# A two-layer encoder trunk on one Trainium2 core: FFN stages in pairs of units with half-contraction weight pieces, and mixer projections with 512 moving columns

## The chip, the cores and the metric

The kernel runs on one core of one Trainium2 chip. The metric is the device time of one execution in microseconds (us). Data starts and ends in HBM. The core's engines work side by side and meet at semaphores: TensorE (PE in the profile, its weight loads PEld), VectorE (DVE), ScalarE (ACT), GpSimd (POOL), SyncE (SP). DMAs are issued here by SyncE (weights) and GpSimd (the conditioning matrices).

## What is computed

One sequence of 256 tokens of 1024 features goes through two layers. Each layer is FFN, mixer, FFN; each of the six sub-layers is

```python
cond = silu(c)
mod = (cond @ ada_w[layer] + ada_b[layer]).reshape(B_, 9, D)   # shift, scale, gate of three sub-layers
h = modulate(rmsnorm(x, norm_g), shift, scale)
x = x + gate * sublayer(h)                                     # 0.5 * gate for an FFN
# swiglu(h): a, b = split(h @ w13); (silu(a) * b) @ w2         w13: 1024 x 5632, w2: 2816 x 1024
```

The mixer of layer 0 projects `h` to six segments of 512 columns (`h @ w_in`), runs differential attention (4 heads) and neighbourhood attention (8 heads) and projects back (`@ w_out`, 1024 x 1024). The mixer of layer 1 takes window means over the tokens and multiplies four groups with 256 x 256 matrices. Everything is float32.

## The kernel before

Weights stream once from HBM; activations stay on the chip. A float32 product is made of three matmuls with rounded operands: an operand v is split into `hi` (a rounded copy, by ScalarE) and `lo` (v - hi, by VectorE), and TensorE adds hi*hi, hi*lo and lo*hi (`three`). All weights and activations of FFNs and projections go through this split: `split_hi`/`split_lo` for w13, w_in, w_out and pool_w, `w2_high`/`w2_low` for w2, `u_high`/`u_low` for the product of the FFN's gate.

An **FFN** works in 22 units of 128 hidden columns. `w13` of a unit: for both halves a and b of w13 and the 8 slices k of the contraction, the 128 x 128 weight block is stationary and the transposed activations `hT` move, 256 tokens: 48 matmuls with 256 columns. a goes to columns 0 to 255 and b to 256 to 511 of PSUM bank 4 + Q % 2. Then ScalarE makes silu(a) (`silu`), VectorE multiplies by b (`u_mul`), both split the product (`u_high`, `u_low`), and `w2` of the unit adds into banks 0 to 3: 12 matmuls with 512 columns. TensorE's order is w13 of unit Q, then w2 of unit Q - 1.

Weights arrive by pairs of units. `raw13` has two slots of 2 MB; a pair's two DMAs (1 MB each, both units, all 8 slices) are issued by SyncE once both units of the pair before the last are split (`lo13_done`). `raw2` has two slots of 0.5 MB; SyncE issues w2 of a unit once the slot's last content is split (`lo2_done`). SyncE's queue is in order: pair, w2, w2, pair, w2, w2. `hi13`/`lo13` and `hi2`/`lo2` have two buffers each. The 22 units are one unit, a turn of four written out, four more turns of an engine loop (`Fori`), and the last unit. Each engine's order within a unit is fixed: ScalarE does `silu`, `w2_high`, `u_high`, `split_hi`; VectorE does `u_mul`, a tile, `u_low`, a tile, `w2_low`, `split_lo`.

The **conditioning vectors** (18, `mod`) are matrix-vector products made by VectorE: eight tiles per vector of 128 x 1024 floats (`ada_tile`, 0.5 MB of DMA each, issued by GpSimd into a ring of four), summed over the partitions by eight transposes on TensorE (`mod_sum`) and a reduction (`mod_out`). Two vectors stand ahead of FFN 0, five are made in each of FFN 0, 1 and 2, one in the mixer, none in FFN 3. The gate is turned into a row over all partitions by a diagonal (`diag`, VectorE), a matmul with ones (`gate_row`) and a copy (`gate_copy`); in the FFNs this stands at the end. The last two w2 tiles and the residual of each FFN are interleaved.

**Norms**: ScalarE squares, GpSimd's power, VectorE's scaling, transposes on TensorE, shift and scale on ScalarE into `h32`, split by VectorE (`norm_split`) slice by slice, `hlo_done` counting slices.

**Mixer of layer 0**: twelve units of 256 columns of w_in (`proj`, 48 matmuls with 256 columns: here a token block of `hT` is stationary and the weights move), both token tiles in one bank, banks 4 and 5 in turn, read out by ScalarE (`win_evac`). Squares, sums, norms, tables and rotations of q and k are woven between the units, and heads 0 to 2 of attention A between the last three. w_out is four such units; the first is cut into four parts around the last heads.

The lines that set the order of one turn before:

```python
# SyncE (turn)                       # TensorE (body)
wait lo13_done; 2 x 1 MB of w13      w13(s, Q, n0 + 1 + d, i4)
wait lo2_done; w2                    if with_mod and d == 3: mod_sum(m0, i)
wait lo2_done; w2                    w2(Q - 1, i4, ...)
```

## Time and profile before

| | us |
|---|---|
| three runs: median (lowest to highest) | 1084.23 (1082.85 to 1085.43) |
| profiled execution: first to last instruction | 1077.9 |
| TensorE busy (modelled ends) | 979.4 |
| VectorE busy | 733.9 |
| ScalarE busy | 441.3 |
| GpSimd busy | 123.6 |

The profiled execution's own time is its span of 1077.9 us; what lies around it in a timed run, starting and ending the program, is the difference of 6.3 us to the median. Rows name engine, source line, operation and the tiles written and read; `x48` is a count. Idle time in brackets names the instruction that ended it. Matmuls overlap, so the distance between two starts, not the duration, is what a matmul takes from TensorE. In the chain of waits each step is followed back to what released it. `raw<-in_ff_w` stands for transfers of w13 and of w2 alike.

### The profile page before, as it was taken

Reading aid. Unit: us, or ns where it says so; the run is one execution under the profiler, and the core shown is the slowest. Engines: PE = TensorE matmul, PEld = TensorE weight load, DVE = VectorE, ACT = ScalarE, POOL = GpSimd, SP = SyncE. Lnnn points to the kernel's source line nnn. Section 1 sums busy time; section 2 is a strip of 40 time slices with the busy share of each in tenths; the row PEclk is TensorE's granted clock in tenths of the full one; section 3 lists DMA queues with packets and bytes.
Section 4 is the critical chain, followed back from the end, with each engine's and each line's share of the span. In section 5 each row is a group of like instructions: output and inputs, shape, how many; then the busy total and the mean of one; then the engine's idle time right before and its main releaser. Section 6 shows DMA issues by size and latency. Waiting matters only on the chain.

```text
span 1077.9 us, 17128 instructions
## 1 busy us (share of the span) xinstructions
PE 979.4 (91%) x6656; PEld 893.6 (83%) x6656; DVE 733.9 (68%) x843; ACT 441.3 (41%) x578; POOL 123.6 (11%) x182
## 2 busy tenths in 40 slices
PE   1598999998979898999999989989999879999998
PEld 1487899997969458998998969879989769999997
DVE  4966778678887544875867867668677675555544
ACT  1424343335536343543444444234333544443432
POOL 1110111102541101110101011101110010000000
PEclk9999999998989699899999989999999989999999
DMA  9986888886734022787887747868787416456441
GB/s 339 343 309 229 277 297 297 290 217 223 242 104 131 1 98 98 269 287 284 282 302 262 270 158 257 308 232 307 277 291 275 149 42 235 164 188 202 148 156 39
DMA packets 155690, 239.19 MB, mean 222 GB/s; under 512 B 14464, under 2 KB 124928, under 8 KB 155520
## 3 DMA queue, kind: packets, MB, share of 16 engines
q1 hardware_dynamic: 135056, 166.81, 46.0%
q0 software_dynamic: 19440, 71.31, 18.2%
q8 instruction: 29, 0.48, 0.2%
q10 hardware_dynamic: 1152, 0.49, 0.2%
q14 instruction: 13, 0.11, 0.0%
HBM read 237.54 MB, written 1.05 MB: 221 GB/s over the span
## 4 chain that ended last, share of the span: by engine, by line
PE 42%; DMA 25%; DVE 18%; issue 6%; ACT 5%; SPq 3%; POOL 1%; ACTq 0%; DVEq 0%; POOLq 0%
PE ps L1106 25%; DMA raw<-in_ff_w 24%; DVE lo L703 6%; DVE acc L744 4%; PE ps L1148 3%; PE ps L1147 3%; PE ps L1151 3%; SPq L296 2%; PE ps L1258 2%; DVE lo L709 1%; DVE x L793 1%; ACT arena L487 1%; PE ps L1261 1%; DVE xn L789 1%; ACT hi L455 1%
## 5 line engine op out<-in xcount | busy, mean ns | idle before, releaser
L1106 PE MATMUL ps<-hT_hi,hi 128*128 128x256 f32 x1408 | 402.0, 286 | 11.1 <-DVE lo L703 6.6
L1106 PE MATMUL ps<-hT_lo,hi 128*128 128x256 f32 x1408 | 400.5, 284 | 0.0
L1106 PE MATMUL ps<-hT_hi,lo 128*128 128x256 f32 x1408 | 400.3, 284 | 0.0
L1106 PEld LDWEIGHTS ps<-hT_hi,hi 128*128 128x128 f32 x1408 | 272.2, 193 | 19.4 <-DVE lo L703 10.5
L1106 PEld LDWEIGHTS ps<-hT_lo,hi 128*128 128x128 f32 x1408 | 272.4, 193 | 2.7
L1106 PEld LDWEIGHTS ps<-hT_hi,lo 128*128 128x128 f32 x1408 | 272.2, 193 | 0.0
L703 DVE TENSOR_TENSOR lo<-raw,hi 128x2048 fp32r<-128x2048 f32 (+1 forms) x110 | 243.8, 2216 | 16.2 <-ACT hi L455 15.5
L455 ACT ACTIVATE hi<-raw 128x2048 fp32r<-128x2048 f32 (+1 forms) x106 | 200.2, 1889 | 31.2 <-DMA raw<-in_ff_w 17.5
L511 ACT ACTIVATE hi<-raw 128x1024 fp32r<-128x1024 f32 x88 | 93.4, 1061 | 276.6 <-DMA raw<-in_ff_w 142.7
L720 DVE TENSOR_TENSOR u_lo<-u_buf,u_hi 128x256 fp32r<-128x256 f32 x88 | 37.3, 424 | 212.6 <-ACT u_hi L504 212.5
L744 DVE SCALAR_TENSOR_TENSOR acc<-ada,cond,acc 128x1024 f32<-128x1024 f32 x115 | 147.0, 1279 | 0.7
L1147 PE MATMUL ps<-hi,u_hi 128*128 128x512 f32 x344 | 138.5, 402 | 1.6 <-DVE u_lo L720 1.6
L1148 PE MATMUL ps<-lo,u_hi 128*128 128x512 f32 x344 | 135.5, 394 | 0.0
L387 POOL DMA_DIRECT2D ada<-in_ada_w x112 | 59.4, 530 | 461.6 <-DVE acc L744 345.0
L709 DVE TENSOR_TENSOR lo<-raw,hi 128x1024 fp32r<-128x1024 f32 x88 | 107.2, 1218 | 0.0
L1151 PE MATMUL ps<-hi,u_lo 128*128 128x512 f32 x344 | 106.7, 391 | 0.0
L499 ACT ACTIVATE s_buf<-ps 128x256 f32<-128x256 f32 x88 | 33.6, 381 | 171.9 <-PE ps L1106 171.7
L1106 PE MATMUL ps<-hi,hT_hi 128*128 128x256 f32 x272 | 80.2, 295 | 5.3 <-DVE lo L703 4.3
L1106 PE MATMUL ps<-lo,hT_hi 128*128 128x256 f32 x272 | 78.0, 287 | 0.0
L1106 PE MATMUL ps<-hi,hT_lo 128*128 128x256 f32 x272 | 77.8, 286 | 0.0
L1151 PEld LDWEIGHTS ps<-hi,u_lo 128*128 128x128 f32 x344 | 64.9, 189 | 14.4
L1147 PEld LDWEIGHTS ps<-hi,u_hi 128*128 128x128 f32 x344 | 65.4, 190 | 13.7 <-DVE u_lo L720 2.0
(126 smaller groups left out, 891.2 us busy)
## 6 DMA issues: line engine op xcount, KB each, us to landing
raw<-in_ff_w SPq DMA_DIRECT2D x86, 1024.0 KB, 7.6
ada<-in_ada_w POOLq DMA_DIRECT2D x132, 512.0 KB, 6.7
raw<-in_ff_w SPq DMA_DIRECT2D x92, 512.0 KB, 8.5
raw<-in_w_in SPq DMA_DIRECT2D x12, 1024.0 KB, 8.0
arena<-in_ada_w SPq DMA_DIRECT2D x4, 1024.0 KB, 18.8
raw<-in_w_out SPq DMA_DIRECT2D x4, 1024.0 KB, 6.3
raw<-in_ada_w SPq DMA_DIRECT2D x2, 1024.0 KB, 15.0
arena<-in_b_rpb SPq DMA_DIRECT2D x16, 128.0 KB, 4.2
```

The lines of the kernel that those rows point to most:

```text
L387: pool.dma_start(ada[:, j % ADA_RING, :], ada_v[layer][:, j, bass.ds(i * D + m0 * D, D)]).then_inc(ada_in[j % ADA_RING], 16)
L455: nc.scalar.activation(hi, src, ACT.Copy).then_inc(hi13_done, 1)
L499: nc.scalar.activation(s_buf[:, Q % 2, :], ps[:, 4 + Q % 2, 0:256], ACT.Silu).then_inc(silu_done, 1)
L511: nc.scalar.activation(hi2[:, Q % 2, :], raw2[:, Q % 2, :], ACT.Copy).then_inc(hi2_done, 1)
L703: ins = V.tensor_tensor(lo, src, hi.bitcast(F32), ALU.subtract)
L709: V.tensor_tensor(lo2[:, Q % 2, :], raw2[:, Q % 2, :], hi2[:, Q % 2, :].bitcast(F32), ALU.subtract).then_inc(lo2_done, 1)
L720: V.tensor_tensor(u_lo[:, Q % 2, :], u_buf[:, Q % 2, :], u_hi[:, Q % 2, :].bitcast(F32), ALU.subtract).then_inc(ulo_done, 1)
L744: V.scalar_tensor_tensor(dst, w, cond[:, j:j + 1], dst, ALU.mult, ALU.add).then_inc(ada_used, 1)
L1106: ins = mm(out, a, b, start=first and m == 0, stop=last and m == len(pairs) - 1)
L1147: mm(ps[:, 2 * t + h, :], uh, wh, start=first, stop=False)
L1148: mm(ps[:, 2 * t + h, :], uh, wl, start=False, stop=False)
L1151: ins = mm(ps[:, 2 * t + h, :], ul, wh, start=False, stop=last)
```

## The change

In the FFNs two units of 128 columns are now worked as a pair (`PAIRS` = 11). Its weights come in two pieces of 1 MB, each with four slices of the contraction for all 256 columns of both a and b; `raw13` is a ring of four such pieces and each piece is freed on its own. `w13(f, p, half)` is 48 matmuls with 256 columns for four slices; a pair takes two banks (`pair_bank`), and pairs alternate between banks 4, 5 and 6, 7. TensorE's order is first half, w2 of the pair before's first unit, (a mod sum or gate row in the spare banks), second half, w2 of its second unit. Silu and product are one operation on 512 elements per pair. Gate rows stand at p = 7 or 9, diagonals at p = 6 or 8; the pool mixer's gate (number 4) is made in FFN 2. The mod sums of alternate vectors use `xn` instead of `acc`. All engine loops are written out. SyncE's order is two pieces, w2, w2; the first w_in piece, the pool weights and the next FFN's first pair are issued before the last w2 of an FFN or right behind it.

In the mixer of layer 0 a projection unit is four slices for 512 columns, so two units make a segment; `proj` has 24 matmuls with 512 columns, one bank per token tile (banks 4 and 5), and a segment's first matmul of a tile waits for `win_evac` of that tile of the segment before. w_out is the same, in four units.

```diff
 def norm_bank(s, j):
-    return ([5, 0, 1, 2] if s == 0 else [5, 0, 1, 4] if s == 4 else [5, 6, 0, 1])[j // 2]
+    return ([0, 1, 2, 3], [6, 7, 0, 1], [0, 1, 4, 5], [6, 7, 0, 1], [5, 0, 1, 4], [4, 5, 0, 1])[s][j // 2]
+def pair_bank(f, p):
+    return 4 + 2 * ((PAIRS * f + p) % 2)
+def spare_bank(f, p):
+    return 4 + 2 * ((PAIRS * f + p + 1) % 2)
-        raw13 = sb("raw13", [P, 2, 2, KT, 256])
+        raw13 = sb("raw13", [P, 4, 2048])
         def unit_src(n):
+            size = 1024 if n // 2 == POOL_PAIR else 2048
+            return raw13[:, n % 4, 0:size], [t[:, n % 2, 0:size] for t in (hi13, lo13)]
...
         def _(sp):
+            def load_piece(n, srcs):
+                if n >= 4:
+                    sp.wait_ge(lo13_done, n - 3)
+                for m in range(2):
...
+            def load_ffn(f, p):
+                for half in range(2):
+                    load_piece(2 * (FFN_PAIR[f] + p) + half,
+                               [w13_v[f][:, 4 * half:4 * half + 4, h * DFF + p * 256:h * DFF + p * 256 + 256]
+                                for h in range(2)])
+                for p in range(PAIRS):
+                    if p < PAIRS - 1:
+                        if (f, p) != (0, 0):
+                            load_ffn(f, p + 1)
...
+                    if (f, p) != (0, 0):
+                        load_w2(f, 2 * p)
+                        load_w2(f, 2 * p + 1)
...
         def _(act):
             def ffn(f):
                 Q0, n0 = NC * f, 2 * FFN_PAIR[f]
+                for p in range(PAIRS):
+                    last = p == PAIRS - 1
+                    if not last or f < 3:
+                        split_hi(n0 + 2 * p + 2)
+                    w2_high(Q0 + 2 * p)
...
+                    silu(f, p)
+                    u_high(Q0 + 2 * p)
+                    if not last:
+                        split_hi(n0 + 2 * p + 3)
+                    w2_high(Q0 + 2 * p + 1)
+                    u_high(Q0 + 2 * p + 1)
...
         def _(dve):
+            def ffn(f):
+                for p in range(PAIRS):
...
+                        ada_tile(g, j)
+                        ada_tile(g, j + 1)
+                    if not last or f < 3:
+                        split_lo(n0 + 2 * p + 2)
+                    w2_low(Q0 + 2 * p)
+                    if f < 3 and p >= 2 and p % 2 == 0 and not last:
+                        mod_out(FFN_MODS[f] + p // 2 - 1, spare_bank(f, p))
+                    if tiles:
+                        ada_tile(g, j + 2)
+                        ada_tile(g, j + 3)
...
+                    u_mul(f, p)
+                    u_low(Q0 + 2 * p)
+                    if not last:
+                        split_lo(n0 + 2 * p + 3)
+                    w2_low(Q0 + 2 * p + 1)
+                    u_low(Q0 + 2 * p + 1)
...
             make_acol(4)
-            diag(GATES[4], 4, 1.0)
...
         def _(pe):
+            def w13(f, p, half):
+                n = 2 * (FFN_PAIR[f] + p) + half
+                pe.wait_ge(lo13_done, n + 1)
+                for kk in range(4):
+                    k = 4 * half + kk
+                    if p == 0:
+                        pe.wait_ge(hlo_done, HLO[SUB_OF_FFN[f]] + k + 1)
...
+            def ffn(f):
+                Q0 = NC * f
+                for p in range(PAIRS):
+                    last = p == PAIRS - 1
...
+                    w13(f, p, 0)
+                    if p >= 1:
+                        w2(Q0 + 2 * p - 2)
+                        pe.wait_ge(u_done, PAIRS * f + p)
+                    if f < 3 and p >= 2 and p % 2 == 0 and not last:
+                        mod_sum(FFN_MODS[f] + p // 2 - 1, spare_bank(f, p))
+                    if f == 2 and p == 7:
+                        gate_row(3, spare_bank(f, p))
+                    if p == 9:
+                        gate_row(4 if f == 2 else SUB_OF_FFN[f], spare_bank(f, p))
+                    if last:
+                        w2(Q0 + 2 * p - 1, tiles=[0], done=None)
+                    w13(f, p, 1)
+                    if last:
+                        w2(Q0 + 2 * p - 1, tiles=[1])
+                    elif p >= 1:
+                        w2(Q0 + 2 * p - 1)
+                if f < 3:
+                    mod_sum(FFN_MODS[f] + 4, spare_bank(f, PAIRS - 1))
                 w2(Q0 + 20, tiles=[0], done=None)
-                gate_row(s, mods)
                 w2(Q0 + 21, tiles=[0], last=True, done=y0_done)
...
+                    if start and kk == 0 and n % 2 == 0 and n >= 2 * WIN_PAIR + 2 and n < 2 * WOUT_PAIR:
+                        pe.wait_ge(win_out, n - 2 * WIN_PAIR - 2 + t + 1)
-                    wh, wl = hi13[:, n % 2, k * 256:k * 256 + 256], lo13[:, n % 2, k * 256:k * 256 + 256]
+                    wh, wl = (v[:, n % 2, kk * 512:kk * 512 + 512] for v in (hi13, lo13))
```

## Rows read from the trace of the kernel before

**Rows 1.** The page: busy time of the engines; GB/s in 40 slices.
```profile
PE 979.4 (91%) x6656; PEld 893.6 (83%) x6656; DVE 733.9 (68%) x843; ACT 441.3 (41%) x578; POOL 123.6 (11%) x182
...
GB/s 339 343 309 229 277 297 297 290 217 223 242 104 131 1 98 98 269 287 284 282 302 262 270 158 257 308 232 307 277 291 275 149 42 235 164 188 202 148 156 39
```
**Rows 2.** Chain of waits, FFN 3: start, duration (us), what.
```profile
1051.38 5.75 PE ps L1106 x48
...
1059.88 5.75 PE ps L1106 x48
```
**Rows 3.** FFNs: stretch, us; busy PE, PEld, DVE, ACT, POOL; clock, DMA, GB/s.
```profile
43.01:247.90 204.89, 197.83 (x1364) 183.95 (x1364) 149.54 (x166) 81.28 (x94) 19.01 (x36) 0.99 0.83 279
434.69:636.00 201.31, 196.45 (x1364) 182.99 (x1364) 147.64 (x157) 88.19 (x99) 19.01 (x36) 0.99 0.78 275
644.39:849.19 204.80, 196.66 (x1365) 182.47 (x1366) 149.15 (x164) 80.51 (x94) 20.57 (x39) 0.99 0.77 273
883.18:1072.70 189.52, 189.32 (x1324) 176.96 (x1324) 99.16 (x106) 79.70 (x93) 0.00 (x0) 1.00 0.46 155
```
**Rows 4.** Timeline, TensorE, FFN 0: a mod sum and the matmul behind it.
```profile
160.99 1.03 PE L1162 MATMUL ps<-ident,acc 128*128 128x128 f32 x8
161.78 0.47 PE L1147 MATMUL ps<-hi,u_hi 128*128 128x512 f32 x1
```
**Rows 5.** Chain of waits, one pair in FFN 1.
```profile
512.49 2.30 DVE lo L703
...
516.24 9.50 DMA raw<-in_ff_w
...
530.00 2.21 DVE lo L703
```
**Rows 6.** Timeline, TensorE, FFN 1: one stop of several.
```profile
495.38 0.39 PE L1106 MATMUL ps<-hT_hi,hi 128*128 128x256 f32 x1 [0.85 <-DVE lo L703]
```
**Rows 7.** Timeline, TensorE and ScalarE, mixer: first read-out; TensorE's stops.
```profile
263.21 0.38 ACT L565 ACTIVATE xn<-ps 128x256 f32<-128x256 f32 x1 [2.85 <-PE ps L1106]
...
300.85 0.36 PE L1106 MATMUL ps<-hi,hT_hi 128*128 128x256 f32 x1 [2.24 <-DVE lo L703]
...
309.11 1.70 PE L1246 MATMUL ps<-ident,xn 128*128 128x128 f32 x8 [2.27 <-DVE xn L926]
...
312.89 0.55 PE L1106 MATMUL ps<-hi,hT_hi 128*128 128x256 f32 x1 [2.08 <-DVE lo L703]
```
**Rows 8.** Groups by shape: splits and tiles; busy us, mean ns, idle before.
```profile
L455 ACT ACTIVATE hi<-raw 128x2048 fp32r<-128x2048 f32 x104 | 198.1, 1905 | 31.2 <-DMA raw<-in_ff_w 17.5 <-PE ps L1106 13.7
L744 DVE SCALAR_TENSOR_TENSOR acc<-ada,cond,acc 128x1024 f32<-128x1024 f32 x115 | 147.0, 1279 | 0.7
L709 DVE TENSOR_TENSOR lo<-raw,hi 128x1024 fp32r<-128x1024 f32 x88 | 107.2, 1218 | 0.0
L511 ACT ACTIVATE hi<-raw 128x1024 fp32r<-128x1024 f32 x88 | 93.4, 1061 | 276.6 <-DMA raw<-in_ff_w 142.7 <-PE ps L1151 133.9
```
**Rows 9.** Timeline, TensorE, first matmuls of FFN 0.
```profile
43.79 0.41 PE L1106 MATMUL ps<-hT_hi,hi 128*128 128x256 f32 x1
44.00 0.41 PE L1106 MATMUL ps<-hT_lo,hi 128*128 128x256 f32 x1
```
**Rows 10.** Timeline, end of FFN 3: silu, gate's row, `u_low`, w2 of unit 21.
```profile
1065.67 0.38 ACT L499 ACTIVATE s_buf<-ps 128x256 f32<-128x256 f32 x1 [4.33 <-PE ps L1106]
...
1066.86 1.88 PE L1170 MATMUL ps<-acc,ones 128*128 128x512 f32 x4
1066.99 0.42 DVE L720 TENSOR_TENSOR u_lo<-u_buf,u_hi 128x256 fp32r<-128x256 f32 x1 [0.48 <-ACT u_hi L504]
...
1068.17 0.79 PE L1147 MATMUL ps<-hi,u_hi 128*128 128x512 f32 x1
```
**Rows 11.** Page: instruction queue; waits of weight loads without a shown releaser.
```profile
q8 instruction: 29, 0.48, 0.2%
...
PEld ps L1106 <- issue: 11.2, 13, 3.7
```

More of the change, by code:

```diff
@@ new lines, in _ @@
+            first_piece(1)
+            load_w2(0, 0)
+            sp.wait_ge(ada_used, KT)
+            load_w2(0, 1)
+            for half in range(2):
+                for h in range(2):
+                    sp.dma_start(raw13[:, 2 + half, h * 1024:h * 1024 + 1024].rearrange("p (k c) -> p k c", c=256),
+                                 w13_v[0][:, 4 * half:4 * half + 4, h * DFF + 256:h * DFF + 512]
+                                 ).then_inc(raw13_in[2 + half], 16)
+            for f in range(4):
+                for p in range(PAIRS):
+                    if p < PAIRS - 1:
+                        if (f, p) != (0, 0):
+                            load_ffn(f, p + 1)
+                    elif f == 0:
+                        load_win(0)
+                    elif f == 1:
+                        load_ffn(2, 0)
+                    elif f == 2:
+                        load_pool()
+                    if (f, p) != (0, 0):
+                        load_w2(f, 2 * p)
+                        load_w2(f, 2 * p + 1)
@@ L380, in _ @@
                 next_rms(1, ss_done, t + 1, slice(t, t + 1))
-            def ada_loop(layer, m0, done, turns):
-                with pool.Fori(0, turns) as i:
-                    for j in range(KT):
-                        pool.wait_ge(ada_used, KT * i + (KT * done + j - ADA_RING + 1))
-                        pool.dma_start(ada[:, j % ADA_RING, :],
-                                       ada_v[layer][:, j, bass.ds(i * D + m0 * D, D)]
-                                       ).then_inc(ada_in[j % ADA_RING], 16)
             def norm_rms(s, halves=False):
@@ L395, in norm_rms @@
                              plus=ss[:, 2:3] if halves and t == 1 else 0.0)
-            ada_loop(0, 2, 2, 5)
+            for g in range(2, 7):
+                ada_vector(g)
             norm_rms(1, halves=True)
@@ L429, in _ @@
             norm_rms(2)
-            ada_vector(8)
-            ada_loop(1, 0, 9, 4)
+            for g in range(8, 13):
+                ada_vector(g)
             norm_rms(3, halves=True)
-            ada_loop(1, 4, 13, 5)
+            for g in range(13, 18):
+                ada_vector(g)
             for n, src in enumerate((pool_b, pool_scale)):
@@ L694, in _, with split_lo @@
             V = nc.vector
-            def split_lo(n, i4=0, part=None):
-                dve.wait_ge(hi13_done, i4 + (n + 1))
+            def split_lo(n, part=None):
+                dve.wait_ge(hi13_done, n + 1)
                 src, (hi, lo) = unit_src(n)
@@ L1136, in w2_last, with w2 @@
                     ins.then_inc(w2_used if h else y1_half, 1)
-            def w2(Q, i4=0, tiles=range(TT), first=False, last=False, done=w2_used):
-                pe.wait_ge(ulo_done, i4 + (Q + 1))
-                pe.wait_ge(lo2_done, i4 + (Q + 1))
+            def w2(Q, tiles=range(TT), last=False, done=w2_used):
+                first = Q % NC == 0
+                pe.wait_ge(ulo_done, Q + 1)
+                pe.wait_ge(lo2_done, Q + 1)
                 p = Q % 2
```

489 lines of the change are left out of this document (208 added, 281 removed).

## Prediction

> **What bounds the kernel now.** I read the page's busy shares first: TensorE is the busiest engine, but 91% is a modelled share [rows 1], so I went on to the chain of waits, to the table by stretch and to the starts of single matmuls. In the last FFN the chain is nothing but TensorE: two units follow each other after 8.50 us, of which 5.75 are the 48 matmuls of w13 with 256 columns (0.120 each) and 2.75 the 12 of w2 with 512 (0.229 each) [rows 2]. The four FFNs take 204.9, 201.3, 204.8 and 189.5 us [rows 3]. The last one builds no conditioning vectors: 22 x 8.50 = 187.0, the gate's row 1.3 and 0.4 in the matmul behind it [rows 10] make 188.7, so it loses 0.8, at its start. The others have five transposed sums in addition, each 0.79 us and 0.1 in the matmul behind it [rows 4]: 189.5 + 4.5 = 194.0. They lose 10.9, 7.3 and 10.8, together 29.0 us.
>
> What they wait for is seen in the chain of FFN 1: the split of a pair's second unit ends; SyncE issues 2 MB of w13 and behind it, in order, w2; the transfer takes 9.5 us; ScalarE rounds w2 and only then does `u_high`; VectorE follows with `u_low`, a tile, the w2 split and the next w13 split, which ends the circle [rows 5]: 17.5 us here and 201.3/11 = 18.3 on the mean, where TensorE needs 17.0 and 0.45 for its share of a sum. ScalarE idles 142.7 us before w2 until a transfer lands [rows 8]. TensorE's own waits are put down to VectorE [rows 6], which had been held up behind `u_low`. In the mixer TensorE stops twice for VectorE's split and once for its rotation, 6.6 us [rows 7].
>
> **The change, FFNs.** Matmuls, weight loads, bytes, tiles and splits are as many as before; their order is new. I lay out one pair from t = 0, the end of its second w13 half. Durations are those of [rows 5, 8, 10]; an operation with 512 elements is 0.6 on ScalarE (0.38 + a quarter of 1.905 - 1.061) and 0.7 on VectorE (0.42 + a quarter of 2.3 - 1.22). TensorE: w2 of the unit before to 2.75, the next first half to 8.5, w2 to 11.25, second half to 17.0. ScalarE: silu to 0.8, `u_high` 2.05, w13 split 3.9, w2 4.9, `u_high` 5.3; next w13 split 8.7 to 10.6, w2 11.5 to 12.5. VectorE: product 1.6, `u_low` 2.5, split 6.2, w2 7.3, `u_low` 7.7, two tiles 10.2, split 12.9, w2 14.0, in every second pair the mod sum 15.4, two tiles 18.0 (that pair lasts 17.9). TensorE wants `u_lo` at 8.5 and has it at 2.5; the second half's split at 11.25, there at 6.2; the next one at 19.75, there at 12.9. The smallest margin is 5 us.
>
> Transfers in the same frame: `w2(2p+1)` is issued when its slot is free at 7.3 - 17 = -9.7 and wanted at 3.9. Both 1 MB pieces go out right behind it (the ring of four has long freed their slots), wanted at 8.7 and 19. `w2(2p+2)` goes out at 14.0 - 17 = -3.0, behind 2.5 MB and the tiles that share the engines; it lands at about +3 and is wanted at 11.5. Each has 8 us in hand where w2 has none today. The stream must bring 5.24 MB (2 MB w13, 1 MB w2, 2 MB tiles) per 17.45 us, 301 GB/s; the slices of FFN 0 reach 343 [rows 1]. So I take all that the transfers cost as gone. FFN 0 keeps 1.6 us: its first 17 matmuls start 0.21 apart instead of 0.12 [rows 9]; the granted clock's column reads 1.00 there all the same, so I only say that TensorE had stood nearly still before and that the change leaves this as it is.
>
> At an FFN's start the first half needs k 0 to 3 only, 1.44 us of matmuls for each instead of 0.72, so 0.5 of the 0.8 lost go; 0.3 stay where the second piece is split behind the norm.
>
> The price is the end of each FFN. Today the last unit's silu, product, `u_high` and `u_low`, 1.7 us [rows 10], lie under w2 of the unit before and the gate's row. After, the chain on 512 elements ends at 2.5 and is covered by half a w2 (1.4) and, except in FFN 3, a mod sum (0.9): 0.2 to 1.1 us idle. Unit 21 then waits for ScalarE's w2 (3.0) and `u_high` (3.4) and VectorE's w2 (4.3) and `u_low` (4.6) where TensorE is ready at 3.9: 0.7. With 0.1 of semaphore time each that is 1.1 us in FFN 0 to 2 and 1.9 in FFN 3. The gate's row moves forward at equal price; the pool's gate row moves from the wait between the stages into FFN 2, +1.7.
>
> FFN 0: 194.0 - 0.5 + 1.6 + 1.1 = 196.2, saves 8.7. FFN 1: 194.6, saves 6.7. FFN 2: 194.6 + 1.7 = 196.3, saves 8.5. FFN 3: 190.9, loses 1.4. Sum 22.5. Half as many silus and products, the w13 splits read in one run instead of strided, the loops' registers: at nothing, since the margins above cover them now as well as after; without that cover each 0.4 us per pair. The diagonal and copy of the pool's gate leave the way between FFN 2 and the pool; at most 0.5, I take 0.
>
> **Mixer projections.** A unit has 24 x 0.229 instead of 48 x 0.120: 5.5 for 5.75. The first unit, whose read-out now starts at 263.2 [rows 7], needs only four k and ends at 261.9; the third ends 1.6 us earlier, and ScalarE has no read-out (0.5) in front of its next split, so the chain of squares, sums and tables moves forward by 2.1. From there VectorE's splits and tables set the end until 312.9 [rows 7], and faster units only lengthen TensorE's waits. Four units behind that give 0.7. I take 2.8. The output projection is bound by TensorE: 168 matmuls at 0.120 become 72 at 0.229, the 12 + 12 among the last heads grow by 2.6, and 0.6 of waiting is filled: 1.8. Together 4.6, bounds 1.5 and 6.6 (no stall left).
>
> The Trainium skill, "TensorE: Matmul & The Clock Gate", section "Back-to-back issue gap", has columns/2.4 + 2.5 ns for the gap, 109 and 216. By it 384 fewer matmuls save 2.7 ns each, 1 us in all; the starts of [rows 2] give 10.6 ns each, 4 us.
>
> New there: each token tile has one PSUM bank instead of two in turn, so a segment's first matmul waits for the read-out of the last segment's first tile. That tile is complete 2.75 us before and its copy takes 0.6. It costs where ScalarE is late (exponentials, `qk_evac` ahead of it in step 8): 0 to 0.7 at five segments, 0 to 3.5; I take 0.
>
> **Sum.** 22.5 + 4.6 = 27.1. The span of 1077.9 becomes 1050.8; the median lies 6.3 above that span: 1084.2 - 27.1 = 1057.1 us.
>
> **Rivals.** (1) The transfers stay late. For: no FFN gets more than 279 GB/s today [rows 3], and tiles share the engines. Against: the engines' share there was 0.83, and SyncE stood in order for much of the rest. If 279 were all, none of the 24 us of FFN 0 to 2 would come: 1081. Half of it: 1069. (2) The single bank costs 3.5: 1060.6. (3) A matmul's fixed part is paid by column, not by instruction, as the formula has it: 3 us less from the mixer, 1060. (4) Slower: code fetching, since TensorE's loops go. Of 6656 matmuls and as many loads [rows 1], 48 units of 120 instructions are repeats; 7552 are left for the 0.48 MB in 29 packets, 64 bytes each [rows 11], so 22 packets are added through engines that are 80% busy. If each stopped TensorE for over 27.1/22 = 1.2 us the kernel would be slower; at the longest idle without a releaser, 3.7 us [rows 11], 81 us are lost: 1138. Against: the mixer and each FFN's first units are straight code already and run without such stops. The same skill, "Runtime: NRT & Kernel Launch", "Instruction fetch mechanics", calls a straight stream's fetch mostly hidden and a taken branch a stall; the loop of FFN 3 shows 8.50 throughout, so I count no gain either. (5) The change does not bring what it says: VectorE, with 15.7 us of work in 17.9, becomes late by as much as w2 was: 1084.
>
> **Chances.** Forecast 0.60 (1051 to 1063); transfers late 0.18 (1063 to 1081); bank 0.07; formula 0.04; VectorE 0.04; code fetch 0.07. The range 1051 to 1072 leaves out the worse half of the first rival and the last two, and a little of the forecast on both sides. A measurement of this kernel tells 0.2%, 2.2 us, from no change: faster 0.89, same 0.04, slower 0.07.
>
> **What would show it.** Right: in FFN 0 to 2 pairs 17.0 and 17.9 apart in turn, ScalarE's wait for w2 transfers under 20 us, TensorE idle only at FFN ends (before w2 of units 20 and 21), FFNs of 196, 195, 196 and 191 us. Rival 1: splits inside FFN 0 to 2 end their wait on a transfer. Rival 2: TensorE waits for a segment's read-out. Code fetch: TensorE idle with no releaser, in FFN 3 too. My reading is wrong altogether if an FFN stays above 200 with its transfers on time.

## The result, and the profile after

The changed kernel takes 1051.63 us (median of 4 runs, 1047.63 to 1066.99), the kernel before on the same chip 1083.54 (1075.36 to 1085.43): 0.9728 of the time, interval 0.9669 to 0.9788 (this ratio leaves out the run of 1066.99, which counts as a slow one). The span of the profiled execution is 1049.6 for 1077.9; the forecast had 1050.8, and 1057.1 for the median. The span came within 1.2 us; two of its parts did not, in opposite directions. The median came out 5.5 us under the forecast, 0.6 above the lower end of its range.

The page of the changed kernel: busy shares, granted clock and GB/s in 40 slices, the instruction queue, and the chain of waits by engine.

```profile
PE 967.8 (92%) x6272; PEld 870.5 (83%) x6272; DVE 737.1 (70%) x799; ACT 433.3 (41%) x529; POOL 123.1 (12%) x182
...
PEclk9999999998989998999999989999999889999999
...
GB/s 340 373 303 328 300 319 284 305 172 261 204 120 121 1 41 203 277 330 343 275 318 267 212 217 232 340 295 325 277 343 159 81 81 191 191 192 170 213 69 61
...
q8 instruction: 50, 0.82, 0.3%
...
PE 83%; DVE 10%; ACT 2%; issue 2%; POOL 1%; DMA 1%; POOLq 0%; ACTq 0%; SPq 0%; DVEq 0%
```

TensorE's busy share was high before too [rows 1]; what changed is the chain that ended last. In the kernel before it was:

```profile
PE 42%; DMA 25%; DVE 18%; issue 6%; ACT 5%; SPq 3%; POOL 1%; ACTq 0%; DVEq 0%; POOLq 0%
```

It lies on TensorE for 83% of the span now, where a round through a transfer and three engines set the pace [rows 5]. The FFNs by stretch, same columns as [rows 3]:

```profile
42.80:239.00 196.20, 195.68 (x1364) 182.90 (x1364) 153.66 (x156) 82.45 (x84) 19.09 (x36) 1.00 0.85 289
415.42:611.35 195.93, 195.45 (x1364) 182.64 (x1364) 151.82 (x147) 81.81 (x84) 19.08 (x36) 0.99 0.82 286
619.83:817.60 197.77, 197.29 (x1368) 183.56 (x1368) 149.98 (x154) 79.85 (x84) 20.72 (x39) 0.99 0.79 280
851.85:1044.30 192.45, 191.10 (x1324) 178.59 (x1324) 96.55 (x94) 77.01 (x81) 0.00 (x0) 0.99 0.47 154
```

They save 8.7, 5.4 and 7.0 us and lose 2.9: 18.2 together, where 22.5 was forecast. (The last window ends 0.2 short of its last matmul; with it the loss is 3.1.) Inside them TensorE runs as laid out. The chain of FFN 3 has two w13 halves 8.50 apart, as in [rows 2]:

```profile
874.01 5.75 PE ps L1107 x48
...
882.51 5.75 PE ps L1107 x48
```

ScalarE's two splits, grouped by shape (busy us, mean ns, idle time before and what ended it), against [rows 8]:

```profile
L440 ACT ACTIVATE hi<-raw 128x2048 fp32r<-128x2048 f32 x104 | 198.5, 1908 | 175.8 <-PE ps L1107 158.4 <-DMA raw<-in_ff_w 17.4
L498 ACT ACTIVATE hi<-raw 128x1024 fp32r<-128x1024 f32 x88 | 92.4, 1050 | 39.0 <-PE ps L1153 36.5 <-DMA raw<-in_ff_w 2.5
```

The 142.7 us of waiting for a w2 transfer are 2.5. ScalarE is idle as much as before, but now it waits for TensorE to free a buffer: the waiting has moved to the engine that isn't the bound.

The rest of the 28.3 us is the mixer. It took 186.8 us (247.9 to 434.7) and takes 176.4 (239.0 to 415.4): 10.4 saved for 4.6 forecast. Most of that is the granted clock, which differs between executions of one program too (e5 below). The stretch of attention A's scores, by windows, in the kernel before (the last three numbers are granted clock, DMA share and GB/s):

```profile
358.00:376.00 18.00, 17.39 (x37) 8.37 (x38) 7.80 (x18) 5.04 (x16) 1.84 (x2) 0.57 0.00 1
```

and in the changed kernel:

```profile
348.00:364.00 16.00, 15.28 (x58) 8.22 (x59) 9.91 (x25) 8.44 (x22) 1.84 (x2) 1.00 0.01 1
```

The same kind of matmuls (37 of them fit into 18 us, 58 into 16), at a granted clock of 0.57 of 2.4 GHz and of 1.00. Two lines of the scores follow each other after 1.15 us in the one and 0.63 in the other.

### The profile page after: what moved, and what is told of

Read it like the earlier page. It is cut to its first block, busy times and chain, and to the rows that moved or that the text cites. A ratio compares the mean times of both kernels' runs of the same rounds, so it can differ in the third digit from the quotient of the medians.

```text
span 1049.6 us, 15172 instructions
## 1 busy us (share of the span) xinstructions
PE 967.8 (92%) x6272; PEld 870.5 (83%) x6272; DVE 737.1 (70%) x799; ACT 433.3 (41%) x529; POOL 123.1 (12%) x182
## 4 chain that ended last, share of the span: by engine, by line
PE 83%; DVE 10%; ACT 2%; issue 2%; POOL 1%; DMA 1%; POOLq 0%; ACTq 0%; SPq 0%; DVEq 0%
PE ps L1107 55%; PE ps L1149 7%; PE ps L1150 7%; PE ps L1153 7%; DVE x L786 1%; DVE lo L694 1%; DVE xn L782 1%; PE ps L1272 1%; PE ps L1162 1%; DVE acc L740 1%; PE ps L1169 1%; PE ps L1275 1%; DMA x<-in_x 1%; POOL rstd L364 1%; DVE xn L740 1%
## 5 line engine op out<-in xcount | busy, mean ns | idle before, releaser
L1149 PE MATMUL ps<-hi,u_hi 128*128 128x512 f32 x344 | 135.3, 393 | 2.8 <-DVE u_lo L714 2.7
L347 POOL DMA_DIRECT2D ada<-in_ada_w x132 | 71.6, 543 | 438.9 <-DVE acc L740 159.8
L484 ACT ACTIVATE s_buf<-ps 128x512 f32<-128x512 f32 x44 | 26.3, 598 | 210.8 <-PE ps L1107 210.8
L740 DVE SCALAR_TENSOR_TENSOR acc<-ada,cond,acc 128x1024 f32<-128x1024 f32 x73 | 93.6, 1282 | 4.5
L708 DVE TENSOR_TENSOR u_buf<-s_buf,ps 128x512 f32<-128x512 f32 x44 | 30.2, 685 | 75.8 <-ACT s_buf L484 75.8
L1150 PEld LDWEIGHTS ps<-lo,u_hi 128*128 128x128 f32 x344 | 64.9, 189 | 10.8
L1107 PE MATMUL ps<-hi,hT_hi 128*128 128x512 f32 (+1 forms) x144 | 58.0, 403 | 5.7 <-DVE lo L694 5.1
L492 ACT ACTIVATE u_hi<-u_buf 128x256 fp32r<-128x256 f32 x88 | 36.1, 410 | 50.0 <-DVE u_buf L708 48.5
```

The source lines that it names most:

```text
L347: pool.dma_start(ada[:, j % ADA_RING, :], ada_v[layer][:, j, v * D:(v + 1) * D]).then_inc(ada_in[j % ADA_RING], 16)
L492: nc.scalar.activation(u_hi[:, Q % 2, :], u_buf[:, Q % 2, :], ACT.Copy).then_inc(uhi_done, 1)
L708: V.tensor_tensor(u_buf[:, :, :].rearrange("p q n -> p (q n)"), s_buf[:, :, :].rearrange("p q n -> p (q n)"), ps[:, pair_bank(f, p) + 1, : ...
L740: V.scalar_tensor_tensor(dst, w, cond[:, j:j + 1], dst, ALU.mult, ALU.add).then_inc(ada_used, 1)
L1107: ins = mm(out, a, b, start=first and m == 0, stop=last and m == len(pairs) - 1, skip_group_check=shared)
L1149: mm(ps[:, 2 * t + h, :], uh, wh, start=first, stop=False)
```

## Experiments: what made the FFNs faster

The theory: in the kernel before, each w2 was issued behind 2 MB of w13 in SyncE's queue, and this, not a lack of bandwidth, bounded the FFNs. The rival: the engines and DMAs were simply at their limit, and pairs, pieces and the ring were needed for it.

**e1_w2_first.** The kernel before, with two lines of SyncE's turn exchanged and nothing else (in each half turn the next two w2 are issued ahead of the next pair):

```diff
+                        for g in range(2):
+                            load_w2_turn(i, 2 + 2 * e + g)
                         sp.wait_ge(lo13_done, 4 * i + (2 * pair - 2))
                         for h in range(2):
                             sp.dma_start(raw13[:, pair % 2, h, :, :],
                                         w13_v[f][:, :, bass.ds(i * 512 + (h * DFF + (2 + e) * 256), 256)]
                                         ).then_inc(raw13_in[pair % 2], 16)
-                        for g in range(2):
-                            load_w2_turn(i, 2 + 2 * e + g)
```

> The kernel before, with one thing moved: in SyncE's turn both w2 transfers are issued ahead of the pair of w13 instead of behind it. Pieces, ring, loops and matmuls stay. My theory (w2 is late because it queues behind 2 MB of w13, and that holds ScalarE and VectorE): w2 lands 8 us earlier than today, the pair is issued one unit (8.5 us) later and still has some 5 us in hand, so most of the 29 us that FFN 0 to 2 lose go: 14 to 22 us faster, ScalarE's wait for w2 transfers falls from 143 us to under 40. Rival (the stream itself is too slow for 17.4 us a pair): no gain, 0 to 3 us, since the bytes are the same, and the wait moves to the w13 splits. Rival (the gain of the change is the finer pieces or the straight code): 0 to 5 us.

Measured: 1053.57 us (median of 5) beside 1076.3 of the kernel before, ratio 0.9809, interval 0.9783 to 0.9836. FFN 0, 1 and 3 by stretch, and ScalarE's w2 split:

```profile
43.00:238.80 195.80, 195.74 (x1364) 183.77 (x1364) 150.13 (x166) 81.51 (x95) 19.00 (x36) 0.99 0.89 291
418.60:612.80 194.20, 194.20 (x1364) 182.21 (x1364) 148.42 (x157) 88.05 (x99) 18.98 (x36) 0.99 0.84 285
...
849.10:1038.70 189.60, 189.60 (x1324) 177.67 (x1324) 99.26 (x106) 79.57 (x93) 0.00 (x0) 1.00 0.47 155
```
```profile
L511 ACT ACTIVATE hi<-raw 128x1024 fp32r<-128x1024 f32 x88 | 93.4, 1061 | 205.1 <-PE ps L1151 196.5 <-DMA raw<-in_ff_w 8.6
```

The theory holds. The order in one queue accounts for the whole of what the change gains in the FFNs: 195.8, 194.2, 195.4 and 189.6 against its 196.2, 195.9, 197.8 and 192.5. It has no price at the end of an FFN, so FFN 3 stays as it was. The bandwidth was there: the same transfers run at 291 GB/s instead of the 279 of [rows 3]. Two limits: 22.7 us by the medians is a little more than the 14 to 22 expected, and the profiled execution is the fastest of the five (1046.00, median 1053.57), so only its stretches are compared here and not its span.

**e3_ring2.** The changed kernel, with the ring of four pieces used as a ring of two:

```diff
                 if n >= 4:
-                    sp.wait_ge(lo13_done, n - 3)
+                    sp.wait_ge(lo13_done, n - 1)
```

> The changed kernel, with SyncE made to wait until the piece two before (not four before) is split, so that only two of the four slots are ever ahead. Worked out in the frame of one pair (0 is the end of its second half): the second piece of a pair can then be issued at -10.8 and w2 of the first unit behind it, which is wanted at -5.5 and lands at about -5; so FFN 0 to 2 lose 0 to 2 us in each of 30 pairs: 5 to 30 us slower. FFN 3, with half the traffic, stays at 191 us. Rival (depth of the ring is not what matters, the order of SyncE's queue is): less than 2 us.

Measured: 1113.59 us (4 runs), ratio 1.0332, interval 1.0277 to 1.0386: 37 us slower than the kernel before, some 60 slower than the changed one. The 5 to 30 us expected were for FFN 0 to 2. These lose some 37 by their stretches (FFN 2 takes 214.4 us); another 22 are lost in the mixer, which the expectation had left out: its weights use the same ring, and the clock was low there for longer. FFN 3 stays, as expected. The w2 split waits longer than it ever did:

```profile
L498 ACT ACTIVATE hi<-raw 128x1024 fp32r<-128x1024 f32 x88 | 92.5, 1051 | 258.5 <-DMA raw<-in_ff_w 252.0 <-PE ps L1153 6.5
```

What SyncE itself waits for (total us, times, longest), in the kernel before (w13), in the changed kernel (w2, then the pieces) and in e3 (the pieces):

```profile
SPq L296 <- DVE lo L703: 420.9, 32, 30.7
...
SPq L269 <- DVE lo L700: 580.1, 82, 13.3
SPq L238 <- DVE lo L694: 234.8, 23, 32.7
...
SPq L238 <- DVE lo L694: 847.1, 100, 41.8
```

So the change cures the same illness as e1 in another way. It leaves w2 behind the pieces in the queue, but the pieces go out right behind the w2 before them, and inside the FFNs SyncE then waits for the slot of w2 (20 or 21 times in each) and for a piece's once at most. With the ring shortened, the queue stands still on a piece's slot and w2 stands behind it, 252 us in all. What e3 doesn't show is that the pairs and the half-contraction pieces bring nothing: it leaves 2 MB of `raw13` in use, where the kernel before had as much as the changed one, 4 MB, and its w2 was late all the same. Whether the pieces' slots, each freed on its own, or the new order of the splits made SyncE's wait for a piece go away, no run here separates.

## Experiments: the granted clock

**e4_keep_busy.** The theory for two remainders (FFN 1 to 3 come out 1.3 to 1.6 us over the forecast; the heads' stretch at 0.57): TensorE stands still around each norm and ahead of the third head, the granted clock falls to 0.5, and what follows starts at half speed. The edit to the changed kernel puts matmuls of no use there, into a bank that is free (24 ahead of a norm, 40 ahead of the last, 6 between token tiles, 24 ahead of the head; none of their results is read):

```diff
+            def keep_busy(bank, n):
+                for _ in range(n):
+                    mm(ps[:, bank, 0:256], u_hi[:, 0, 0:P], u_hi[:, 1, :], start=True, stop=True)
             def norm(s):
...
                 for t in range(TT):
+                    if busy:
+                        keep_busy(busy[0], busy[1] if t == 0 else 6)
                     pe.wait_ge(xn_done, 2 * s + t + 1)
...
             qk_transpose(1, 0)
+            pe.wait_ge(win_out, 12)
+            keep_busy(4, 24)
             weights_transpose(3)
```

> The changed kernel with idle matmuls added, 24 of 256 columns (40 before the last FFN) into a bank nobody uses, where TensorE waits for the norms and for head 3. Nothing waits for their result. In the changed kernel the granted clock is at its lower level at the start of each of FFN 1 to 3, whose first 144 matmuls take 19.0 to 19.3 us instead of 17.3. Theory: the loss at an FFN's start is the clock, and it falls because TensorE stands still in the norm; then the first 144 matmuls take 17.3 to 17.6 us and the kernel is 4 to 8 us faster. Rival (the start is paced by the split of the normed activations): no change at the starts, and the added matmuls cost up to 1 us at each of five places.

Measured: 1042.43 us, ratio 0.9694, interval 0.9671 to 0.9718, and all five runs within 1.7 us of each other (1041.40 to 1043.07). Beside the changed kernel (e5 below, on another chip, ratio 0.9772) that is 8 us by the ratios and 10 by the medians, where 4 to 8 were expected. A second time on another chip, **e9_keep_busy_again**:

> The changed kernel with TensorE kept busy around the norms and ahead of the third head, once more, as the base of the next three: their differences are 1 to 5 us, and only with the granted clock held can such be read. It should take 30 to 35 us less than the kernel before, within 2 us from run to run.

Measured: 1042.99 (1041.40 to 1043.33), ratio 0.9669, interval 0.9642 to 0.9697. The start of FFN 1, its first 144 matmuls, in the changed kernel:

```profile
415.41:434.45 19.04, 19.04 (x144) 19.04 (x145) 15.06 (x18) 9.58 (x12) 2.11 (x4) 0.90 0.93 325
```

and with TensorE kept busy (e9), with the windows of its mixer (from the first projection on) and of FFN 1 to 3:

```profile
414.53:432.36 17.83, 17.59 (x144) 17.38 (x145) 15.40 (x18) 10.06 (x12) 2.12 (x4) 1.00 1.00 361
...
247.82:414.53 166.71, 153.31 (x714) 113.73 (x715) 118.18 (x170) 78.65 (x138) 42.24 (x30) 0.97 0.38 127
414.53:609.40 194.87, 194.15 (x1366) 181.30 (x1367) 151.92 (x147) 82.00 (x85) 19.16 (x36) 1.00 0.82 288
617.40:813.50 196.10, 195.59 (x1369) 182.03 (x1370) 150.22 (x154) 80.02 (x86) 20.82 (x39) 1.00 0.81 283
844.80:1036.00 191.20, 189.59 (x1324) 176.75 (x1324) 96.73 (x95) 77.00 (x81) 0.00 (x0) 1.00 0.47 155
```

At full clock the first 144 matmuls take 17.83 instead of 19.04, and FFN 1 to 3 come to 194.9, 196.1 and 191.2: the forecast's 194.6, 196.3 and 190.9 within 0.3. The theory holds. Between the two profiled executions (1049.6 and 1041.1) 4.5 us are gained in FFN 1 to 3, 2.8 between FFN 2 and FFN 3, 1.5 between FFN 0 and FFN 1 and 0.3 between FFN 1 and FFN 2, and 0.7 lost in FFN 0, which has no idle matmuls. The clock isn't held everywhere: 0.97 over the mixer is still some 10 us at half speed.

**e5_after_again.** The changed kernel, unaltered:

> The changed kernel itself, unaltered, beside the others on the same chip, as their base. It should take 22 to 30 us less than the kernel before. The scatter of its runs tells how large the share of the granted clock is: the theory that low stretches of the clock around the norms and ahead of the attention heads explain the 1.3 to 1.6 us by which FFN 1 to 3 miss the forecast expects a scatter of several us between runs here, while the kernel that keeps TensorE busy in those places had one of 1.7 us.

Measured: 1052.81 us (7 runs, 1051.77 to 1064.98) beside 1076.12, ratio 0.9772, interval 0.9734 to 0.9810: 23 us. Its profiled execution is the one of 1064.98. Six runs lie within 1.6 us and this one 12 above; its mixer and its heads show why:

```profile
238.80:434.20 195.40, 172.82 (x677) 121.92 (x677) 125.45 (x180) 82.78 (x147) 47.12 (x38) 0.83 0.34 116
348.00:394.00 46.00, 45.18 (x114) 23.10 (x112) 17.00 (x44) 14.68 (x40) 1.84 (x2) 0.57 0.07 23
```

The low clock lasted 41 us here, 3.4 in the first profile of the same kernel, and the mixer is 19.0 us longer (195.4 for 176.4), half of the 37.6 more at half speed. It is chance in a program that doesn't change: the same matmuls after the same stops. The FFNs scatter with it, the other way: FFN 1 and 3 of this execution, and the first 144 matmuls of FFN 1:

```profile
434.16:629.04 194.88, 194.41 (x1364) 181.64 (x1364) 151.84 (x147) 81.85 (x84) 19.08 (x36) 1.00 0.81 288
866.88:1057.92 191.04, 189.46 (x1324) 176.81 (x1324) 96.58 (x94) 76.97 (x81) 0.00 (x0) 1.00 0.47 155
434.16:452.14 17.98, 17.98 (x144) 17.98 (x145) 15.07 (x18) 9.59 (x12) 2.11 (x4) 0.96 0.97 345
```

With no idle matmuls at all they are within 0.3 of the forecast here, at a clock of 0.96 behind the norm instead of 0.90; FFN 2, at 197.2, is not.

**e7_before_keep_busy.** The same edit in the kernel before (14 matmuls ahead of the pool's norm, and none between its token tiles):

> The kernel before with matmuls of no use put on TensorE while it waits for the norms and ahead of the third head (24, 40 at the last norm, 6 between token tiles). If the heads' stretch of the mixer was 7.7 us longer before only because the granted clock was low there, that stretch goes from 40.5 to about 33 us, and starts of FFN 1 to 3 shorten by 1 to 2 us each where they are not waiting for transfers: 8 to 12 us faster than the kernel before. The four FFNs keep their waits for w2 (some 200 to 205 us for FFN 0 to 2). Rival: the heads' stretch is slow for a reason of its own (the order of units before it): no more than 3 us.

Measured: 1073.82 us (12 runs, 1071.64 to 1078.28), ratio 0.9981, interval 0.9956 to 1.0007: 2 us, not clear of noise and 5 at the most, where 8 to 12 were expected. Its mixer, from the first projection on, and FFN 1:

```profile
257.61:427.35 169.74, 157.15 (x1098) 136.51 (x1099) 120.45 (x171) 78.24 (x139) 42.35 (x30) 0.97 0.40 131
427.35:632.50 205.15, 195.77 (x1366) 181.46 (x1366) 147.63 (x157) 88.43 (x100) 19.00 (x36) 1.00 0.77 270
```

The mixer did what was expected: from 247.9:434.7 to 249.5:427.35 it is 8.9 us shorter. Two things ate it. FFN 1 took 205.15 us instead of 201.31, FFN 0 206.5 instead of 204.9, both still waiting for w2: where the transfer sets the pace, a faster start of TensorE only lengthens its wait. And the profiled execution of before is not typical of this kernel. Of its 17 runs beside this one 13 lie between 1071.9 and 1079.4 and four between 1082.3 and 1085.3, so most of them probably didn't have its 17 us of low clock in the heads; that last step is inferred, since they have no trace. Their mean granted clocks agree with it: 0.952 to 0.962 in the four, 0.960 to 0.981 in the 13.

**e8_w2_first_keep_busy.** e1 and e7 together, nothing of the change:

> The kernel before with both small edits and nothing of the change: w2 issued ahead of the next pair of w13 in SyncE's turn, and matmuls of no use around the norms. If the two act in different places (waits for w2 inside the FFNs; the granted clock at their starts and in the heads) the gains add: 20.5 + 10 = about 30 us faster than the kernel before, at or below the changed kernel. If the clock was low because TensorE stood still for w2, the second edit adds nothing to the first: 20 us.

Measured: 1042.76 us (6 runs), ratio 0.9686, interval 0.9647 to 0.9724. The 33 us are more than the sum of the two alone (23, on another chip, and 2), which fits e7: the clock's gain counts only once TensorE is the bound. Two small edits to the kernel before are 10 us faster than the changed kernel and as fast as the changed kernel with its clock held.

## Experiments: the parts of the forecast

**e2_proj256.** The changed kernel, with every projection matmul of 512 moving columns made as two of 256:

```diff
-                    ins = three(out_of(t), ((hh, wh), (hh, wl), (hl, wh)), start and kk == 0, stop and kk == 3)
+                    for c in range(2):
+                        cs = slice(c * 256, c * 256 + 256)
+                        ins = three(out_of(t)[:, cs], ((hh, wh[:, cs]), (hh, wl[:, cs]), (hl, wh[:, cs])),
+                                    start and kk == 0 and c == 0, stop and kk == 3, shared=True)
```

> The changed kernel, with each projection matmul of 512 columns made as two of 256; order, pieces, banks and waits stay. By the spacing of starts (0.120 and 0.229 us) a unit takes 5.75 instead of 5.5 us: 2.8 us slower in w_in (the rest under VectorE's chain) and 1.0 to 1.8 in w_out, 2.5 to 4.5 us in all, 0.2 to 0.4%. If the fixed part were paid by column only, 1 us or less. If the mixer's gain is something else (the granted clock among the heads of group B), the projections' stretch grows by these numbers and the heads' stretch takes a length of its own, 33 us with the clock up, 40 us with it down.

Measured: 1058.88 us (6 runs, 1054.42 to 1069.75), ratio 0.9863, interval 0.9822 to 0.9904. It can't be read: its profile had 20.5 us of low clock in the heads, which by e5's measure is 8 to 9 us more than the first profile of the changed kernel had, and the runs scatter over 15. So it was done again with the clock held.

**e10_keep_busy_proj256.** e9 with the same edit:

> As e9, with each projection matmul of 512 moving columns made as two of 256. The forecast had 4.6 us for the 512 columns (2.8 in w_in, 1.8 in w_out); the trace of the changed kernel gave some 1.0 up to the heads and about 1.8 in w_out. If the forecast's sum holds, this is 4.6 us slower than e9; if VectorE's splits and tables take back what TensorE gains in w_in, it is 2.5 to 3.7 slower, and TensorE's stops before the heads are shorter by what its units are longer. Rival: the price of a matmul goes by columns alone, and the difference is under 1 us.

Measured: 1043.81 us (6 runs, 1042.89 to 1045.48), 0.8 over e9, and in the mixer 0.9 (167.57 for 166.71):

```profile
248.01:415.58 167.57, 154.92 (x1098) 134.15 (x1099) 118.13 (x170) 78.50 (x138) 40.72 (x30) 0.98 0.38 126
```

That is the rival's number, but not for the rival's reason. Matmuls with 512 columns do save their fixed part: the first five units of w_in take 27.7 us for 29.1 (a mod sum of 0.79 among them taken off), and 72 matmuls of w_out 16.85 for 17.49 as 144. Up to the heads VectorE takes back most of it: TensorE's first wait for a split, at 290.7 us, is 2.87 in e9 and 2.01 in e10, and from the first projection to the first scores it is 100.3 for 100.9. (The wait for a rotation behind it, 1.00 and 2.34, can't be read in this way: it is 2.62 and 1.01 in two executions of the unaltered kernel.) From e7 to e9, both at a clock of 0.97, the stretch goes from 169.74 to 166.71, 3.0 us, of which the columns are 0.9. The other 2.1 must come from what else the change does in the mixer; I hold it to be the half-contraction pieces, but no run takes them out alone.

**e6_tail.** The changed kernel, with the gate rows of FFN 0, 1 and 3 put back to the end of the FFN (ScalarE's copy of the row and TensorE's wait for it move along, not shown):

```diff
-                    if p == 9:
-                        gate_row(4 if f == 2 else SUB_OF_FFN[f], spare_bank(f, p))
+                    if p == 9 and f == 2:
+                        gate_row(4, spare_bank(f, p))
...
                 if f < 3:
                     mod_sum(FFN_MODS[f] + 4, spare_bank(f, PAIRS - 1))
+                if f == 3:
+                    gate_row(5, spare_bank(f, PAIRS - 1))
                 w2(Q0 + 20, tiles=[0], done=None)
+                if f < 2:
+                    gate_row(SUB_OF_FFN[f], pair_bank(f, PAIRS - 1))
                 w2(Q0 + 21, tiles=[0], last=True, done=y0_done)
```

> The changed kernel with the gate rows of FFN 0, 1 and 3 moved back to the end of the FFN: in FFN 3 the row stands between the last w13 half and w2 of unit 20, in FFN 0 and 1 between w2 of unit 20 and w2 of unit 21. If the end of an FFN costs what the trace shows (TensorE idle 0.4 to 0.5 us before w2 of unit 21 in FFN 0 to 2, 0.93 + 0.41 in FFN 3), the gate's row of 1.3 us fills it: FFN 0 and 1 shorter by 0.4 each, FFN 3 by 1.3, the kernel by 2.1 us. Rival: the copy of the gate's row by ScalarE and the wait of the residual for it come out late instead, and the gain is 0 or it is up to 1 us slower.

Measured: 1046.10 us (6 runs, 1043.88 to 1058.69), ratio 0.9726, interval 0.9674 to 0.9778: 6.7 under e5. Three times what was expected, with the clock's scatter in both (four runs near 1045, two near 1058). Once more with the clock held, **e11_keep_busy_tail**:

> As e9, with the gate rows of FFN 0, 1 and 3 moved back to the end of the FFN. The stops before w2 of units 20 and 21 (0.4 in FFN 0 and 1, 0.93 + 0.41 in FFN 3) should be filled: 2.1 us faster than e9, 1040.3 where e9 takes 1042.4. If instead the whole 7 us between the two kernels without idle matmuls came from the tail, it would be 7 us faster; I hold most of those to be the granted clock.

Measured: 1038.47 us (6 runs, 1037.92 to 1040.12), ratio 0.9631, interval 0.9605 to 0.9658: 4.5 under e9 by the medians, 2.8 by the spans. The end of FFN 3 in the changed kernel, timeline of TensorE (start, duration, what, idle time before):

```profile
1038.15 0.50 PE L1149 MATMUL ps<-hi,u_hi 128*128 128x512 f32 x1 [0.93 <-DVE u_lo L714]
...
1040.24 0.50 PE L1149 MATMUL ps<-hi,u_hi 128*128 128x512 f32 x1 [0.41 <-DVE u_lo L714]
```

and in e6:

```profile
1043.94 0.62 PE L1153 MATMUL ps<-hi,u_lo 128*128 128x512 f32 x2
1044.40 1.88 PE L1169 MATMUL ps<-arena,ones 128*128 128x512 f32 x4
1045.71 0.79 PE L1149 MATMUL ps<-hi,u_hi 128*128 128x512 f32 x1
```

With the gate's row between them (1.31 from start to start) both stops are gone. From its start, or its norm's transposes, to the next norm's or the end, FFN 0 is 0.8 shorter than in e9, FFN 1 0.7 and FFN 3 1.7. I had expected 0.4, 0.4 and 1.3 from the idle times shown; the matmul behind a stop starts slowly too, its successor 0.34 later instead of 0.23, and that isn't in the bracket. FFN 3 comes to 189.6:

```profile
843.70:1033.30 189.60, 189.33 (x1324) 176.85 (x1324) 96.84 (x95) 77.03 (x82) 0.00 (x0) 1.00 0.48 156
```

The medians differ by 1.7 us more than the spans because the profiled execution of e11 is the slowest of its six (1040.12), while that of e9 lies at its median. It is also the only one of the six with a mean granted clock of 0.982; the other five read 0.995 to 0.997 and have spans of 1036.1 to 1037.5. In e9 four read 0.981 (spans 1041.1 to 1041.5) and two 0.995 and 0.996 (1039.6). Compared like with like the gate rows are worth about 3 us.

**e12_keep_busy_tail_start.** e11 with matmuls on the identity ahead of FFN 0 too:

```diff
             norm(0)
+            keep_busy_at_start(28)
             mod_sum(0)
+            keep_busy_at_start(34)
             pe.wait_ge(mod_red, 1)
             mod_sum(1)
+            keep_busy_at_start(11)
             ffn(0)
```

> As e11, with idle matmuls on the identity between the first norm, the first two conditioning sums and FFN 0 as well (28, 34 and 11 of 128 columns). The forecast kept 1.6 us for the slow first matmuls of FFN 0 and left open why they are slow. If the granted clock is the cause, their starts go from 0.21 to 0.12 apart and the kernel gains 1.2 to 1.6 us over e11. If transfers or the first touch of the data are the cause, the starts stay 0.21 apart and nothing is gained. If the idle matmuls hold the second conditioning sum up, up to 1 us is lost.

The stretch ahead of FFN 0, its first 2.3 us and its first 144 matmuls, in e11:

```profile
18.00:42.98 24.98, 3.92 (x17) 3.18 (x17) 22.99 (x23) 3.41 (x5) 2.22 (x4) 0.57 1.05 390
42.98:45.30 2.32, 2.32 (x11) 2.32 (x12) 2.08 (x6) 2.32 (x6) 0.00 (x0) 0.50 1.04 378
42.98:62.82 19.84, 19.84 (x144) 19.84 (x145) 15.19 (x18) 10.19 (x12) 2.12 (x4) 0.86 0.98 322
```

and in e12:

```profile
18.00:42.75 24.75, 20.58 (x161) 20.07 (x161) 22.75 (x23) 3.41 (x5) 2.22 (x4) 0.93 1.05 391
42.75:45.10 2.35, 2.35 (x19) 2.35 (x20) 2.11 (x6) 2.35 (x6) 0.00 (x0) 1.00 1.03 377
42.75:60.81 18.06, 17.60 (x145) 17.40 (x145) 15.49 (x18) 10.57 (x12) 2.12 (x4) 1.00 1.06 370
```

The clock was the cause: 0.50 and 1.00 at the first matmuls, their starts 0.21 and 0.12 apart, 1.8 us less for the same 144, the same GB/s. The span is 1.5 shorter (1036.8 for 1038.3). But the medians are equal, 1038.42 (6 runs, 1037.49 to 1040.70) and 1038.47, and so are the medians of the six spans, 1036.65 both: the 1.5 is measured from e11's slowest execution, the one at 0.982. The other five of e11 may have started FFN 0 at the high clock by themselves; they have no trace, so this stays open.

## Why the prediction was right, and where it wasn't

**What bounds the kernel: right.** The circle through w2's transfer cost the 10 us per FFN, and e1 shows it by the smallest possible edit. I had worked out how late the transfer is and left unasked what the cheapest way around it would be.

**FFN 0: exact**, 196.2, though to the tenth only by luck: it is 195.9 in e5 and 196.9 in e9, whose code there is the same. Pairs are 17.0 apart, 17.9 with a mod sum, as laid out, and the split of w2 waits 2.5 us for transfers.

**FFN 1 to 3: 1.3, 1.5 and 1.6 too low.** The step that failed is the one on an FFN's start ("so 0.5 of the 0.8 lost go"): I read the loss at an FFN's start as matmuls waiting for slices of the norm and gave back 0.5 of 0.8. The first 144 matmuls of FFN 1 to 3 take 19.0 to 19.3 us where 17.3 would be TensorE's pace. It is the granted clock after the norm, 0.90 over that stretch; with it held they take 17.8, 17.3 and 17.8, and the FFNs are within 0.3 of the forecast. Part of the miss is this one execution: in e5 the same three starts take 18.0, 18.6 and 17.8. In [rows 9] I had the slow starts before me and didn't tie them to it, because the clock's column reads 1.00 there. The record of that execution holds no value before that time, and the column shows full clock where there is none; in e11 it has them and reads 0.50. Spacing is the better witness: 0.21 for 256 columns is 1.2 GHz.

**The tail's price: about right.** 1.1 (FFN 0 to 2) and 1.9 (FFN 3) were forecast; putting the gate rows back recovers 0.8 (FFN 0), 0.7 (FFN 1) and 1.7 (FFN 3). The stop before unit 20 is hidden by the mod sum in FFN 0 to 2 and is 0.93 in FFN 3. What the forecast didn't say: this price is a choice of where the gate's row stands, and not one of pairs.

**Mixer: 4.6 forecast, 3.0 with the clock held, 10.4 in the profiles.** Of w_in's 2.8, 1.5 came (e7 to e9, 101.8 to 100.3 us up to the scores): the chain of VectorE behind the first units moves forward by less than the 2.1 I gave it, and the first stop grows to 2.87 where [rows 7] has 2.24. The second, 2.62 for 2.27, is no sign of it, since it was 1.01 in e5. In the changed kernel:

```profile
290.88 0.50 PE L1107 MATMUL ps<-hi,hT_hi 128*128 128x512 f32 x1 [2.87 <-DVE lo L694]
...
299.23 1.46 PE L1260 MATMUL ps<-ident,xn 128*128 128x128 f32 x8 [2.62 <-DVE xn L927]
```

Of w_out's 1.8, 1.5 came: 21.1 us become 16.85, and the two pieces among the last heads grow by 2.7 (forecast 2.6). The other 7.4 us are put down to the clock in the heads, 20.5 us of low clock in one profiled execution and 3.4 in the other; half of the 17.1 between them is 8.5, so the two parts don't add up to better than 1 us. The forecast took the profiled execution of before as the kernel and had no term for that.

**The sum.** 18.2 instead of 22.5 in the FFNs, 10.4 instead of 4.6 in the mixer: 28.3 with the 0.3 the rest lost, forecast 27.1. Two misses cancel, and both are the granted clock: that the span came within 1.2 us is luck. On the second chip, where before's median run lies 7 us lower, the same change is worth 23 us; with the clock held in both (e7 to e9, two chips), 31 by the medians and 29 by the spans.

**The median: 5.5 too high.** The step that failed is "the median lies 6.3 above that span". Every run with both numbers on record shows some 2.1 us between time and span in the kernel before and 1.8 in the changed one (1051.39 and 1049.6 for the profiled execution). So the profiled execution of before took some 1080.0 and was 4 us faster than the three timed ones: 4.5 us of the miss are this term and 1.2 the span. By the spans the change was forecast as 27.1 and measured as 28.3; by the medians it is 31.9.

**Small slips.** By the cited formula two matmuls of 256 columns cost 2.5 ns more than one of 512, not 2.7, and 5.24 MB in 17.45 us are 300 GB/s, not 301; nothing hangs on either.

**Rivals.** Transfers late (1): not so, 2.5 us of waiting before w2, slices of up to 373 GB/s; e3 shows what it would have looked like. Single bank (2): no wait for a read-out among TensorE's stops. Fixed part by column (3): refuted, 0.229 for 512 columns and 0.120 for 256 in all profiles. Code fetching (4): the packets are there, 50 for 29, 21 more with 22 forecast, and they cost nothing that can be seen: FFN 3 keeps 8.50 per unit throughout, as its loop did, and the idle time of these weight loads without a releaser is 11.7 us for the 11.2 of [rows 11]. VectorE late (5): not so; TensorE waits for VectorE's splits of w13 and w_in 5.1 us in all, in two places, both in the mixer.

## What to carry to other kernels

When small transfers that are wanted soon share an in-order queue with large ones that are not, exchange the two before rebuilding anything: two lines moved did for the FFNs here what pairs, pieces and a ring of four did. Read the granted clock of every stage in both profiles before explaining a difference; it moved one stage by 19 us from one execution to another of the same program. A gain off the bound counts only once the bound is gone: idle matmuls gave 2 us alone, within the noise, and 11 on top of the exchange.

## What the runs showed of the hardware

The granted clock has two levels in all records here, 1.0 and 0.5. It was low after stops of TensorE: at each norm, where it waits 3.2 us for the first transposes and again behind them, and in the heads, which begin behind a stop of 3.0 us. How long it stayed low there differed between executions of one program, 3.4 and 41 us. The nearest rule is that of the Trainium skill, "TensorE: Matmul & The Clock Gate", "What's actually happening": it calls the slow phase at a kernel's start variable from run to run and puts its cost under 1% of a typical span. The first agrees with e5. The second doesn't hold for slow phases in mid-kernel here: 37.6 us more of it were 19 us, 1.8%.

Matmuls of no use, 24 at a norm (40 at the last) and ahead of one head, held the clock up there, took 10 us off the time (1052.8 to 1043.0, on two chips) and reduced the scatter of the runs from 13 us to 2. TensorE stood idle there otherwise.

The fastest kernel of the study is the changed one with idle matmuls and the gate rows at the end, 1038.47 us, 0.9631 of the kernel before; e12's idle matmuls at the start add nothing to it that the times show.
